# Sixty-four candidate pairs in the expert retrieval, and weighted token-innermost one-hots as the stationary operand of the spread

## What is computed

```
s = einsum('thpd,hpkd->thpk', q, sub_keys)            # 8 heads, 2 sets of 128 sub-keys
s_top, i_top = top_k(s, 16)
cand_s = s_top[.., 0, :, None] + s_top[.., 1, None, :]      # 16 x 16 sums
cand_i = i_top[.., 0, :, None] * 128 + i_top[.., 1, None, :]
best_s, best_pos = top_k(cand_s, 16)
idx = take_along_axis(cand_i, best_pos);  g = softmax(best_s)
h = einsum('td,ted->te', x, u[idx]);  out = einsum('te,ted->td', gelu(h) * g, v[idx])
```

## Time and profile before

| | us |
|---|---|
| median of 3 runs (lowest, highest) | 3316.73 (3316.06, 3318.95) |
| profiled execution: its time, its span | 3322.88, 3321.2 |
| busy in the span: PE, DVE, ACT, POOL | 3068.7, 2621.2, 1005.1, 1286.2 |

### The profile page before, as it was taken

How to read it: one execution, slowest core, us unless ns; L and a number is a source line. 1 busy time by engine, 2 the same in 40 slices (tenths; PEclk the granted TensorE clock), 3 DMA queues, 4 the chain that set the end, 5 groups by cost and what they waited for, 6 DMA issues and landing times. The chain is left out here.

```text
span 3321.2 us, 50919 instructions
## 1 busy us (share of the span) xinstructions
PE 3068.7 (92%) x17450; PEld 1716.5 (52%) x17450; DVE 2621.2 (79%) x5543; ACT 1005.1 (30%) x1471; POOL 1286.2 (39%) x891
## 2 busy tenths in 40 slices
PE   8898899889888499999986999999999999999999
PEld 4444555445444266666653555555555554444444
DVE  3235455429999999999967888888888888999996
ACT  4322255333332255554522222222222222222221
POOL 1021111012432322111226666666655555556652
PEclk9998557999999799999997999999999999999999
DMA  3210100121110144444448887888888888888885
GB/s 106 64 38 1 51 1 1 45 83 59 54 51 34 51 160 166 172 178 161 182 183 293 294 275 275 279 290 274 275 281 283 272 273 278 305 297 305 296 297 181
DMA packets 256173, 594.90 MB, mean 179 GB/s; under 512 B 20768, under 2 KB 127408, under 8 KB 252976
## 3 DMA queue, kind: packets, MB, share of 16 engines
q1 hardware_dynamic: 180016, 318.63, 28.4%
q0 software_dynamic: 73728, 268.47, 22.8%
q10 hardware_dynamic: 2304, 6.29, 0.5%
HBM read 513.63 MB, written 79.69 MB: 179 GB/s over the span
## 5 line engine op out<-in xcount | busy, mean ns | idle before, releaser
L238 PE MATMUL f_y<-f_v_hi,f_a_hi 128*128 128x512 f16 x1536 | 583.3, 380 | 11.8 <-DVE p_h L2172 11.7
L239 PE MATMUL f_y<-f_v_lo,f_a_hi 128*128 128x512 f16 x1536 | 583.2, 380 | 0.0
L240 PE MATMUL f_y<-f_v_hi,f_a_lo 128*128 128x512 f16 x1536 | 583.2, 380 | 0.0
L2139 POOL DMA_INDIRECT f_rows<-in_peer_u,p_row_index x256 | 353.3, 1380 | 211.8 <-DVE f_rows L2180 129.4
L2139 POOL DMA_INDIRECT f_rows<-in_peer_v,p_row_index x256 | 311.0, 1215 | 281.8 <-DVE p_h L2190 253.6
L2180 DVE SCALAR_TENSOR_TENSOR f_rows<-f_rows,p_xs 128x1024 f32<-128x1024 f32 x256 | 380.0, 1517 | 49.3 <-DMA f_rows<-in_peer_u,p_row_index 49.2
L2190 DVE SCALAR_TENSOR_TENSOR p_h<-f_rows,f_row_a,p_h 128x1024 f32<-128x1024 f32 x256 | 394.7, 1542 | 18.7 <-DMA f_rows<-in_peer_v,p_row_index 11.9
L2172 DVE SCALAR_TENSOR_TENSOR p_h<-f_y,p_h 128x512 f32<-128x512 f32 x384 | 263.0, 685 | 106.6 <-PE f_y L240 104.4
L2150 POOL TENSOR_TENSOR f_v_lo<-f_v_in,f_v_hi 128x1024 f16<-128x1024 f32 x128 | 282.1, 2204 | 144.1 <-ACT f_v_hi L2114 143.0
L238 PE MATMUL f_hid<-p_act_hi,x_u_hi 128*128 128x384 f16 x1008 | 330.2, 328 | 2.0 <-DVEq L2157 2.0
L239 PE MATMUL f_hid<-p_act_lo,x_u_hi 128*128 128x384 f16 x1008 | 330.2, 328 | 0.0
(11 more groups left out here) (299 smaller groups left out, 5606.3 us busy)
## 6 DMA issues: line engine op xcount, KB each, us to landing
f_v_in<-in_peer_v SPq DMA_DIRECT2D x128, 512.0 KB, 5.2
dense_weights<-e_stage SPq DMA_DIRECT2D x24, 2048.0 KB, 8.7
f_g_in<-dense_weights SPq DMA_DIRECT2D x32, 1536.0 KB, 15.7
x_u_in<-in_peer_u SPq DMA_DIRECT2D x64, 512.0 KB, 4.8
e_u_in<-in_peer_u SPq DMA_DIRECT2D x48, 512.0 KB, 4.2
x_gel<-early_tiles SPq DMA_DIRECT2D x64, 384.0 KB, 3.5
early_tiles<-e_gel SPq DMA_DIRECT2D x48, 384.0 KB, 2.5
a_w_in<-in_w_in SPq DMA_DIRECT2D x24, 512.0 KB, 3.9
```

The lines of the kernel that those rows point to most:

```text
L238: pe.matmul(out, a_hi, b_hi, start=first, stop=False)
L239: pe.matmul(out, a_hi, b_lo, start=False, stop=False)
L240: return pe.matmul(out, a_lo, b_hi, start=False, stop=last)
L2139: nc.gpsimd.indirect_dma_start(out=rows[q % ROWS][:], out_offset=None, in_=table, in_offset=bass.IndirectOffsetOnAxis(ap=T.row_index[:, ti ...
```

## The change

In the retrieval only those pairs are added that can be among the 16 best: since both lists are sorted, the pair (a, b) has (a + 1)(b + 1) - 1 pairs ahead of it. The rows 0, 1 to 3, 4 to 7 and 8 to 15 of the first list are paired with the first 16, 8, 4 and 1 of the second: 64 sums in four additions, and the second `top16` works on 64 elements. A position is turned back into its two ranks by arithmetic on 128 elements in float32. The match matrices are laid out with the rank outermost, so that both inputs and the output of the comparison are float16 with step 1 (`ranks`, `match`); the sum over the rank then reads with a step of 256 bytes. The reciprocal comes ahead of the comparisons, and the multiplication of the weights (L1714) goes to GpSimd, behind its two multiplications of match matrices.

In the spread the key-2 one-hot is compared once for 4 tokens in float16 with the tokens innermost (`same`), and multiplied twice by the halves of the weights (`left`, now with two parts, still the stationary operand, read with a step of 4 elements, 8 bytes). The key-1 one-hot (`right`) is unweighted, one instruction of 512 elements, and moves. Four instructions a step stand in place of nine.

```diff
+PAIRINGS = ((0, 1, 16), (1, 3, 8), (4, 4, 4), (8, 8, 1))
+NCAND = sum(n * width for _, n, width in PAIRINGS)
-        cand = S.sb("cand", [P, NT, TOPK * TOPK])
+        cand = S.sb("cand", [P, NT, NCAND])
-        match = S.sb("match", [P, 2, NT * TOPK, TOPK], F16)
+        match = S.sb("match", [P, 2, TOPK, NT * TOPK], F16)
@@ retrieve, gpsimd
-                    got = match[:, n].rearrange("p (t k) a -> p t k a", t=NT)
-                    nc.gpsimd.tensor_tensor(got, got, top_f[:, b, :, n, :].unsqueeze(2).broadcast_to(
-                        [P, NT, TOPK, TOPK]), ALU.mult).then_inc(matched, 1)
+                    got = match[:, n].rearrange("p a (t k) -> p a t k", t=NT)
+                    nc.gpsimd.tensor_tensor(got, got, top_f[:, b, :, n, :].rearrange("p t a -> p a t").unsqueeze(
+                        3).broadcast_to([P, TOPK, NT, TOPK]), ALU.mult).then_inc(matched, 1)
+                pool.wait_ge(total_done, h + 1)
+                nc.gpsimd.tensor_tensor(picked[2][:, :, bass.ds(h * TOPK, TOPK)], weight[:],
+                                        lanes(total[:], 2, P, NT, TOPK), ALU.mult).then_inc(weight_done, 1)
@@ retrieve, vector
-                c.step(nc.vector.tensor_tensor(
-                    cand[:].rearrange("p t (a b) -> p t a b", a=TOPK),
...
+                for a, n, width in PAIRINGS:
+                    c.step(nc.vector.tensor_tensor(
+                        cand[:, :, at:at + n * width].rearrange("p t (a b) -> p t a b", a=n),
...
+                if not (first and b == 0):
+                    dve.wait_ge(weight_done, h)
                 nc.vector.tensor_tensor(weight[:], best[:], best[:, :, 0:1].broadcast_to([P, NT, TOPK]),
                                         ALU.subtract).then_inc(shifted, 1)
-                c.step(nc.vector.tensor_scalar(part[:, 0, :], pos[:], 4, None, ALU.logical_shift_right))
-                c.step(nc.vector.tensor_scalar(part[:, 1, :], pos[:], TOPK - 1, None, ALU.bitwise_and))
+                c.step(nc.vector.tensor_scalar(part[:, 0, :], pos[:], 3, None, ALU.logical_shift_right))
+                c.step(nc.vector.tensor_scalar(part[:, 1, :], pos[:], 2, None, ALU.logical_shift_right))
+                c.step(nc.vector.tensor_copy(pos_f[:], pos[:]))
                 c.wait()
-                c.step(nc.vector.tensor_copy(part_f[:], part[:]))
+                c.step(nc.vector.tensor_scalar(row[0][:], part[:, 0, :], -1.0, 0.0, ALU.add, ALU.max))
                 if not (first and b == 0):
                     for n in range(2):
                         index_sum(h - 1, n)
                 c.wait()
+                c.link(nc.vector.scalar_tensor_tensor(row[1][:], part[:, 1, :], -6.0, row[0][:], ALU.add, ALU.max))
+                c.link(nc.vector.scalar_tensor_tensor(row[2][:], pos_f[:], -48.0, row[1][:], ALU.add, ALU.max))
+                c.step(nc.vector.tensor_scalar(start[0][:], row[2][:], 8.0, 8.0, ALU.mult, ALU.add))
+                c.step(nc.vector.tensor_scalar(start[1][:], row[2][:], 4.0, 24.0, ALU.mult, ALU.add))
+                c.step(nc.vector.tensor_copy(part_f[:, 0, :], row[2][:]))
+                c.wait()
+                c.step(nc.vector.scalar_tensor_tensor(start[2][:], row[2][:], 16.0, start[0][:], ALU.mult, ALU.min))
+                c.step(nc.vector.scalar_tensor_tensor(start[3][:], row[2][:], 48.0, start[1][:], ALU.add, ALU.min))
+                c.wait()
...
+                    nc.vector.tensor_tensor(match[:, n], lanes(part_f[:, n, :], 1, P, TOPK, NT * TOPK), ranks[:],
                                             ALU.is_equal).then_inc(found, 1)
+                c.link(nc.vector.tensor_tensor(start[4][:], start[2][:], start[3][:], ALU.min))
+                c.link(nc.vector.tensor_tensor(part_f[:, 1, :], pos_f[:], start[4][:], ALU.subtract))
                 dve.wait_ge(weighted, h + 1)
                 c.link(nc.vector.tensor_reduce(total[:], weight[:], AX.X, ALU.add))
-                c.link(nc.vector.reciprocal(total[:], total[:]))
-                nc.vector.tensor_tensor(picked[2][:, :, bass.ds(h * TOPK, TOPK)], weight[:],
-                                        lanes(total[:], 2, P, NT, TOPK), ALU.mult).then_inc(weight_done, 1)
+                nc.vector.reciprocal(total[:], total[:]).then_inc(total_done, 1)
+                for n in range(2):
+                    find(n)
@@ spread_weights, vector
-                    for j in range(BANK_T):
-                        tok = bass.ds(blk * BLOCK + (s * BANK_T + j), 1)
-                        nc.vector.tensor_scalar(right[r][:, 0, j, :], iota[:], key1_t[:, tok], w_hi[:, tok],
-                                                ALU.is_equal, ALU.mult)
...
+                    nc.vector.tensor_tensor(same[s % 2][:], iota[:], each(key2), ALU.is_equal).then_inc(same_done, 1)
                     dve.wait_ge(spread, BASE - RING + 1 + blk * STEPS + s)
+                    nc.vector.tensor_tensor(right[r][:], lanes(T.iota[:], 1, P, BANK_T, P),
+                                            lanes(key1_t[:, toks], 2, P, BANK_T, P), ALU.is_equal)
+                    dve.wait_ge(same_done, blk * STEPS + s + 1)
+                    nc.vector.tensor_tensor(left[r][:, 0], same[s % 2][:], each(w_hi), ALU.mult)
+                    nc.vector.tensor_tensor(left[r][:, 1], same[s % 2][:], each(w_lo), ALU.mult).then_inc(built, 1)
@@ spread_weights, tensor
-                            mm = pe.matmul(tab[r][:, j, :], left[r][:, j, :], right[r][:, part, j, :],
+                            mm = pe.matmul(tab[r][:, j, :], left[r][:, part, :, j], right[r][:, j, :],
                                            start=part == 0, stop=part == 1)
```

More of the change, by code:

```diff
@@ L1370, in retrieve @@
         part = S.sb("part", [P, 2, NT * TOPK], U32)
+        pos_f = S.sb("pos_f", [P, NT * TOPK])
+        row = [S.sb(f"row{n}", [P, NT * TOPK]) for n in range(3)]
+        start = [S.sb(f"start{n}", [P, NT * TOPK]) for n in range(5)]
+        ranks = S.sb("ranks", [P, TOPK, NT * TOPK], F16)
         part_f = S.sb("part_f", [P, 2, NT * TOPK], F16)
@@ L1392, in retrieve @@
         weighted = S.sem("weighted")
+        ranks_done = S.sem("ranks_done")
         found = S.sem("found")
@@ L1633, in _ @@
                                            ALU.subtract).then_inc(w_lo_done, 1)
+            nc.vector.tensor_copy(ranks[:], lanes(T.iota[:, 0:TOPK], 2, P, TOPK, NT * TOPK)).then_inc(ranks_done, 1)
             def top16(c, groups):
@@ L1671, in index_sum @@
                 out = picked[n][:, :, bass.ds(h * TOPK, TOPK)]
-                nc.vector.tensor_reduce(out, match[:, n].rearrange("p (t k) a -> p t k a", t=NT), AX.X,
+                nc.vector.tensor_reduce(out, match[:, n].rearrange("p a (t k) -> p t k a", t=NT), AX.X,
                                         ALU.add).then_inc(index_done, 1)
-            STEPS = 140
+            STEPS = 152
             def step(hh, b, first=False):
@@ L1747, in spread_weights @@
         E = EarlyTiles(nc, io, T, S, EARLY_S, EARLY_R * PEER_H, EARLY_S * NBLOCK)
-        iota = S.sb("iota", [P, P], F16)
-        left = [S.sb(f"left{r}", [P, BANK_T, P], F16) for r in range(RING)]
-        right = [S.sb(f"right{r}", [P, 2, BANK_T, P], F16) for r in range(RING)]
-        w_hi16 = S.sb("w_hi16", [P, DSEQ], F16)
-        w_hi = S.sb("w_hi", [P, DSEQ])
+        iota = S.sb("iota", [P, P, BANK_T], F16)
+        same = [S.sb(f"same{r}", [P, P, BANK_T], F16) for r in range(2)]
+        left = [S.sb(f"left{r}", [P, 2, P, BANK_T], F16) for r in range(RING)]
+        right = [S.sb(f"right{r}", [P, BANK_T, P], F16) for r in range(RING)]
+        key2, w_hi, w_lo = (S.sb(n, [P, DSEQ], F16) for n in ("key2", "w_hi", "w_lo"))
         stage = [S.sb(f"stage{b}", [P, NKEYS, TB]) for b in range(2)]
@@ L1773, in _ @@
             c = Chain(dve, vec_step)
[L1774 to L1778 removed]
+            c.step(nc.vector.tensor_scalar(w_t, w_t, S_G, None, ALU.mult))
+            c.step(nc.vector.tensor_copy(iota[:], lanes(T.iota[:], 2, P, P, BANK_T)))
+            c.link(nc.vector.tensor_copy(key2[:], key2_t))
+            c.link(nc.vector.tensor_copy(w_hi[:], w_t))
+            c.link(nc.vector.tensor_tensor(w_lo[:], w_t, w_hi[:], ALU.subtract))
             with dve.Fori(0, NBLOCK) as blk:
```

31 lines of the change are left out of this document (13 added, 18 removed).

## The result

The changed kernel takes 3207.76 us (median of 4 runs, 3202.43 to 3208.9) against 3317.84 in the same company: a ratio of 0.9665 [0.9649, 0.9682]. The forecast was 3203, with a range of 3192 to 3260.

The account below looks back on a forecast made before the run. VectorE was taken to bound retrieval and spread, TensorE the experts, with TensorE bounding both changed stages afterwards. Profiled 3322.9 - 70 (retrieval) - 44 (spread) = 3208.9 us, less 6.2 for the median: 3203 us, range 3192 to 3260.

Parts of the forecast that it names:

- The bound of the retrieval: Retrieval: TensorE takes over from VectorE as the bound; steps of 42.2 us instead of 50.7, stage -70 us.
- VectorE's step: Retrieval: VectorE's work a step falls from 50.8 to 40.0 us, or 37.8 with fast comparisons.
- the fast value: Retrieval comparisons: 16-bit ones at the cast's rate, 1.15 us each, against 2.25 if no faster.
- the strided sums: Retrieval index sums (L1672): left at 4.48 us for both, with an upper bound of twice that, +4.5 us.
- a wait of 4 to 5 us for the exponential: Retrieval: VectorE arrives at 32 us of TensorE's step and waits 4 to 5 us for ScalarE, done at about 36.8.
- Rival 1: Retrieval: VectorE still bounds it, strided sums double (+4.5 us), comparisons gain nothing; 46.6 us a step, kernel 3233 us; 10%.
- the four stops of 2.15 us a block: Spread: VectorE stops behind four `low` of 2.15 us in each 16-step block, 8.6 us, making 34.5 or 47.0 us.
- Two-input operations of VectorE and GpSimd's thus exclude each other: Retrieval: inferred from VectorE's 128-element weights' multiplication, 3.49 us behind GpSimd's match multiplication against 0.29 in L1695.
- 3: Rival, spread: the gapped weight load is slower, up to 0.117 us; kernel 3250 us with half, 3297 with all; 15%.
- 4: Rival, spread: the gapped load takes four times the columns' time, 0.222 us, 255 us in all; kernel 3458 us; 3%.
- 2: Rival, spread: 16-bit operations run no faster; spread 564 us, 16 more than before, kernel 3263 us; 8%.
- 5: Rival, retrieval: the multiplication moved to GpSimd takes over 15 us more a step, `low` comes late; about 3240 us; 2%.

Follow-up runs that it names:

- sums_twice: Changed kernel with each index sum of the retrieval run twice, the first time into an unread buffer; 3267.91 us, ratio 0.9843.
- slow16: Changed kernel with the spread's key-2 comparison in float32, so all VectorE operations there have a four-byte operand; 3343.69 us, ratio 1.0065.
- guard: Changed kernel where VectorE, after its first step of the spread, waits for GpSimd's first low half; 3205.42 us, ratio 0.9663.
- slow16_gap: Changed kernel with the spread's four-byte operands, plus VectorE waits that make gaps for GpSimd's low parts; 3309.43 us, ratio 0.9979.
- all16: Changed kernel with 16-bit operands also in the spread's first-key comparison, so in all four operations; 3208.60 us, ratio 0.9674.
- r_alone: The new retrieval with the old spread, against the kernel before; 3249.83 us, ratio 0.9795.
- old_layout: Changed kernel with match matrices laid out as before: rank innermost, adjacent sums, comparison against the float32 ramp; 3216.69 us, ratio 0.9699.
- quarter_sums: Changed kernel with the retrieval's index sums over only four of sixteen ranks; 3202.03 us, ratio 0.9645.
- step64: Changed kernel with the spread's stationary one-hots interleaved, weight loads reading columns 64 bytes apart instead of 8; 3221.22 us, ratio 0.9703.

## Why the prediction was right

**The bound of the retrieval: right.** The step came out at 42.33 us against 42.2 and the stage at -70.6 against -70. The sum of TensorE's own pieces from the earlier trace rows was the right way to get it: the wait of 6.03 us went away, and the rest stayed. The last step took 51.9 us (52.8).

**VectorE's step: right in kind, one term mis-sized.** Second top16 7.2 us (871.59 to 878.82; 6.8 forecast), pair sums 0.89 (0.85), comparisons 1.22 us each, so the fast value (1.15). The chain of nine operations lasts 2.46 us (886.97 to 889.43) against 2.4. The term that failed is the strided sums, of which I wrote "I leave as they are": 7.31 us, not 4.48. My upper bound had been +4.5, and +2.8 is what it is. I had taken the low end because no row showed a sum paying for its step, though no row had a sum with a step either. The step that followed from it, a wait of 4 to 5 us for the exponential, came out at 0.3 us once in the whole stage. The time of that exponential was right: it was done at 889.28, which is 36.7 us into TensorE's step (its turn at 852.62), against 36.8. Rival 1 had this term in it, at +4.5, and sums_twice shows how near it was: another 1 us or so a step on VectorE, and VectorE would have set the time.

The rule of the Trainium skill on lines of 16 bytes (Advanced Engine Details and Errata, section SBUF Cachelines) was right in direction for the sums: at 256 bytes a factor of 1.62 (3.69 against 2.28 us). It gives no size, and rival 1, which I had put down to it, needed more than it says: sums of twice the time and comparisons that gain nothing. For the load the rule held nearly: at 8 bytes the load is 15 ns longer and the matmuls no further apart, at 64 bytes they are 0.008 us further apart. In neither case did it decide the result.

**The spread's steady state: right.** Four steps on TensorE:

```profile
1302.74 1.06 PE L1851 MATMUL e_tab<-e_right,e_left 128*128 128x128 f16 x16
1303.64 1.04 PE L1301 MATMUL e_u_ps<-p_ident,e_u_in 128*128 128x128 f32 x8
1308.42 1.06 PE L1851 MATMUL e_tab<-e_right,e_left 128*128 128x128 f16 x16
1313.21 1.00 PE L1851 MATMUL e_tab<-e_right,e_left 128*128 128x128 f16 x15
```

From 1302.74 to 1313.21 it is 10.47 us against 10.48 forecast, where the earlier trace rows has 11.43. Two of VectorE's groups in the middle of the spread, beside those of the earlier trace rows:

```profile
L1832 DVE TENSOR_TENSOR e_left<-e_same,e_w_hi 128x512 f16<-128x512 f16 x161 | 67.0, 416 | 0.0
L1829 DVE TENSOR_TENSOR e_right<-p_iota,p_picked_all 128x512 f16<-128x512 f32 x162 | 117.1, 723 | 149.4 <-PE e_tab L1851 149.4
```

416 ns where I had read 0.42 us from the cast of the earlier trace rows. VectorE is 63% busy, not 80%: the four stops of 2.15 us a block that I had charged it are nearly absent. L1829's mean of 723 ns is 45 ns above the 678 of an undisturbed one; ten of its 192 take 1.33 us. For the whole spread that is under 9 us, where I had charged 8.6 to each of its twelve blocks. It costs nothing here, but the idea behind it was wrong, as the next point says.

**Where it was off: the start of the spread, and who stops for whom.** I had taken off 2 us for the start; it was 8.6, and this is nearly the whole of what the spread missed (6.6 of 7.3 us, -36.7 against -44). The step that failed is "Two-input operations of VectorE and GpSimd's thus exclude each other", read as VectorE paying. In the kernel before VectorE was busy without a break too, yet GpSimd's first low part took 2.13 us and a VectorE operation beside it 2.24:

```profile
1162.83 2.24 DVE L1791 TENSOR_SCALAR e_right<-e_iota,p_picked_all 128x128 f16<-128x128 f16 x1
...
1162.89 2.13 POOL L1317 TENSOR_TENSOR e_u_lo<-e_u_all,e_u_hi 128x1024 f16<-128x1024 f32 x1 [15.32 <-ACT e_u_all L1311]
```

All 48 low parts of that spread fall on such an operation, one with a single wide input, which then takes 2.1 to 2.2 us instead of 0.30. With nothing but two-input operations in a row it is GpSimd that stays out, until the run ends. The short operation with one wide input thus stops for GpSimd too, and what sets the two-input ones apart is that GpSimd doesn't get in between them. No run had a stream of long operations with one input or of short ones with two, so that it is the second input and not the length that matters is argued and not shown. The Trainium skill, SBUF — State Buffer, section Who interferes with whom, says that such operations contend and that issue order decides; it speaks of one instruction, while these traces show whole runs of them (14.3 us).

**The rivals.** 3 and 4 were priced from four-byte rows; at the 8 bytes of this change the matmuls are no further apart, and even 64 bytes cost an eighth of the 0.061 us a matmul. 2 was mis-sized most: with operations at four-byte speed the spread takes 641 us, not 564, since the price had stops of VectorE in it and none of TensorE behind `low`. It would have made the kernel slower than before, so the 8% that I gave it belonged to the other sign, and slower should have had 11% instead of 3. 5 had no part in it: GpSimd's two multiplications take 8.5 us and the weights' 0.40, inside the bounds given.

**The sum.** The profiled execution was forecast at 3208.9 us and took 3208.9; that is luck: the front was 5.5 us shorter without an edit and the gap 1.1 us, which I had put at nothing, against 7 us that the spread fell short. The median lies 4.8 us above the forecast. I had carried over the 6.2 us between profile and median of the kernel before; in the changed kernel they are 1.1 us apart. The front of that profile, 741.5 us, is with slow16's the longest of all, which is the likely reason; no other execution of the kernel before was cut into stages.

## What to carry to other kernels

Work out what the next engine needs with its waits taken away; that sum gave the steps of both stages within 0.2 us, and it also said how much of VectorE's 300 us would count. Then ask of every engine with gaps what it does for others in them: a stream of two-input VectorE operations without a break can cost more through the GpSimd operation that it keeps out than by its own length, and waits in the right places, costing VectorE time that it doesn't need, give some of it back (5.6 us of the spread in guard, 30 of the 130 in slow16_gap). A layout that makes one operation fast makes another slow, so price all that read the buffer, and compare small edits by stage where untouched stages vary more than they are worth.

## What was unexpected of the hardware

- A GpSimd operation of 2.13 us lasted 6.29 (the changed kernel), 7.02 (all16) and 14.33 us (slow16) beside runs of VectorE's two-input operations, and ended 1.97 to 1.98 us after the last of the run in all three cases. Runs with the 128-element operations of one wide input (r_alone, before) never showed this: the longest low part of the spread before took 2.85 us.
- A comparison of 512 elements with 16-bit operands only (all16) takes 0.42 us when both run over adjacent elements and 0.69 us when one is repeated along the innermost dimension.
- A sum over 16 elements that lie 256 bytes apart takes 3.69 us for 2048 f16 elements, against 2.28 us for adjacent ones (old_layout); for 512 elements, four to a sum, it takes 1.03 us (quarter_sums).
- A load of 128 f16 columns takes 98, 113 and 150 ns at steps of 2, 8 and 64 bytes; only the last (step64) moves the matmuls apart, from 0.056 to 0.064 us.
